# Joined products in a Strassen feed-forward: matmuls sorted by columns, a fourth joined product, and sums moved to GpSimd

## What is computed

```python
xn2 = rms_norm(h, norm2_w[l])
h = h + (jax.nn.silu(xn2 @ w_ffn_gate[l]) * (xn2 @ w_ffn_up[l])) @ w_ffn_down[l]
return rms_norm(h, final_norm_w)
```

## Time and profile before

| | us |
|---|---|
| median of 3 runs | 815.28 (815.2 to 820.14) |
| profiled execution | 815.42 |
| its span, first to last instruction | 813.7 |
| TensorE matmuls busy in it | 807.3 (99%) |
| VectorE | 561.7 (69%) |
| ScalarE | 441.3 (54%) |
| GpSimd | 413.6 (51%) |

### The profile page before, as it was taken

One profiled execution on the slowest core, in us unless ns is written; L12 is line 12 of the kernel. 1 busy time (PEld: TensorE's weight loads), 2 busy tenths in 40 slices (PEclk: granted clock), 3 DMA queues, 4 the chain that ended last, 5 costly groups with the idle time before them and its releaser, 6 DMA issues.

```text
span 813.7 us, 12790 instructions
## 1 busy us (share of the span) xinstructions
PE 807.3 (99%) x5192; PEld 734.2 (90%) x5192; DVE 561.7 (69%) x600; ACT 441.3 (54%) x501; POOL 413.6 (51%) x146
## 2 busy tenths in 40 slices
PE   9999999999999999999999999999999999999997
PEld 8888888888888899999998899999999999999985
DVE  5377377364774957888974278777778888878836
ACT  5523446756665645867442575544555446665624
POOL 3545424424224543477955443544444445878880
PEclk9999999999999999999999999999999999999999
DMA  8972422131122253322235302332234445536022
GB/s 290 269 272 107 158 101 101 55 103 53 52 104 106 102 207 105 104 104 105 84 131 204 104 1 104 136 108 109 109 110 160 161 159 188 183 121 216 2 77 104
DMA packets 29869, 103.11 MB, mean 127 GB/s; under 512 B 2816, under 2 KB 7296, under 8 KB 25856
## 3 DMA queue, kind: packets, MB, share of 16 engines
q1 hardware_dynamic: 24592, 87.07, 30.1%
q10 hardware_dynamic: 5232, 15.40, 6.0%
HBM read 94.08 MB, written 8.39 MB: 126 GB/s over the span
## 4 chain that ended last, share of the span: by engine, by line
PE 99%; ACT 0%; issue 0%; DVE 0%; ACTq 0%
PE acc L2170 11%; PE acc L2172 11%; PE acc L2173 11%; PE acc L1955 7%; PE acc L1957 6%; PE acc L1956 6%; PE acc L2182 6%; PE acc L1972 6%; PE acc L1973 6%; PE acc L1974 6%; PE acc L2184 3%; PE acc L2400 3%; PE acc L2001 3%; PE acc L2388 2%; PE acc L2390 2%; PE acc L2391 2%
## 5 line engine op out<-in xcount | busy, mean ns | idle before, releaser
L489 POOL TENSOR_TENSOR w_lo<-raw,w_hi 128x2048 fp32r<-128x2048 f32 x26 | 122.7, 4718 | 163.3 <-ACT w_hi L684 163.3
L510 POOL TENSOR_TENSOR A_lo<-wp,A_hi 128x1024 fp32r<-128x1024 f32 x51 | 126.0, 2470 | 144.3 <-ACT A_hi L859 137.2
L874 ACT ACTIVATE S_hi<-acc 128x1024 fp32r<-128x1024 f32 x68 | 68.1, 1025 | 90.2 <-PE acc L2173 39.7
L1477 DVE TENSOR_TENSOR S_lo<-acc,S_hi 128x1024 fp32r<-128x1024 f32 x68 | 81.7, 1219 | 14.2 <-ACT S_hi L874 14.1
L1955 PE MATMUL acc<-xt_hi,w_hi 128*128 128x512 f32 x224 | 88.0, 393 | 0.0
L1957 PE MATMUL acc<-xt_hi,w_lo 128*128 128x512 f32 x224 | 87.2, 389 | 0.0
L1956 PE MATMUL acc<-xt_lo,w_hi 128*128 128x512 f32 x224 | 87.2, 389 | 0.0
L684 ACT ACTIVATE w_hi<-raw 128x2048 fp32r<-128x2048 f32 x26 | 49.6, 1910 | 63.9 <-PE acc L1974 43.5
L859 ACT ACTIVATE A_hi<-wp 128x1024 fp32r<-128x1024 f32 x51 | 53.8, 1054 | 17.6 <-PE acc L2173 17.6
L2182 PE MATMUL acc<-ft,A_hi 128*128 128x512 f32 x144 | 51.7, 399 | 0.0
L1957 PEld LDWEIGHTS acc<-xt_hi,w_lo 128*128 128x128 f32 x224 | 42.0, 188 | 8.8
(11 more groups left out here) (362 smaller groups left out, 2608.6 us busy)
## 6 DMA issues: line engine op xcount, KB each, us to landing
wp<-wstream SPq DMA_DIRECT2D x34, 1024.0 KB, 7.0
raw<-wstream SPq DMA_DIRECT2D x26, 1024.0 KB, 4.8
wd<-wstream SPq DMA_DIRECT2D x16, 512.0 KB, 6.2
down_sums<-act_sum ACTq DMA_DIRECT2D x8, 512.0 KB, 3.2
sum_raw<-down_sums SPq DMA_DIRECT2D x8, 512.0 KB, 3.8
xn_in<-x ACTq DMA_DIRECT2D x4, 512.0 KB, 8.3
turned_sums<-tx ACTq DMA_DIRECT2D x4, 512.0 KB, 3.9
raw_out<-wstream SPq DMA_DIRECT2D x2, 1024.0 KB, 5.8
```

The costliest lines, as they stand in the source:

```text
L489: pool.tensor_tensor(w_lo[s][:, :], raw[s][:, :], w_hi[s][:, :], ALU.subtract).then_inc(lo_ready, 1)
L510: pool.tensor_tensor(low_of(name, rows), weights_of(name, c, rows), high_of(name, rows), ALU.subtract).then_inc(plain_low, 1)
L874: a.activation(high_of(name, rows), src, ACT.Copy).then_inc(op_high, 1)
L1477: v.tensor_tensor(low_of(name, rows), src, high_of(name, rows), ALU.subtract).then_inc(s_low, 1)
```

## The change

1. In `wide_product` and `wide_down_product` all matmuls of 512 columns come first, then all of 256 columns.
2. In pairs 9 to 17 four products are joined: A11 and S2 in banks 6 and 7 (now `SPARE`), S3 and A22 in banks 1 and 2 (`LAST_ROW`). A12 is plain, in bank 0; S1 and S4 are plain in bank 3. The down pairs keep their three joined products and their banks.
3. u3 and C21 are joined by two VectorE instructions each, C11 by one straight from bank 0 without ScalarE's copy. P1's join moves ahead of S4's forming.
4. The high and the low part of S3 come before C21 and before S1's, in pairs 8 to 16.
5. TensorE: A11 waits for a low part of S (S3's, since it uses those banks), S1 for the second one; S2 waits for P1's join; A12 for the C11 of the pair before; the first down pair's A11 also for C21 of pair 17.
6. `act_sums` moves from VectorE to GpSimd, at the end of GpSimd's pair.

```diff
-        FIRST_ROW, SECOND_SUM = (0, 1), (6, 7)
+        FIRST_ROW, LAST_ROW, SPARE = (0, 1), (1, 2), (6, 7)
...
+            def act_sums(q):
+                m = (q - FIRST_SUMS) // 2
...
+                if q == FIRST_SUMS:
+                    pool.wait_ge(act_ready, 2)
+                    pool.wait_ge(pair_ready, 3)
+                    pool.tensor_tensor(t1, x12, x11, ALU.subtract).then_inc(t_formed, 1)
+                    pool.wait_ge(t_formed, A_FORMED + 1)
+                    pool.tensor_tensor(t2, x22, t1, ALU.subtract).then_inc(t_formed, 1)
...
                 pair((None, p), p % 2)
+                if p < LAST_FFN:
+                    act_sums(p - MERGE_PAIRS)
...
-                    a.activation(by_bank(p1), low_sums(FIRST_ROW), ACT.Copy).then_inc(low_taken, 1)
+                    a.wait_ge(joined, at(p, 5, 1 - 10))
+                    a.wait_ge(taken, at(p, 2, -2))
+                    a.activation(by_bank(p1), low_sums(SPARE if spare else FIRST_ROW), ACT.Copy).then_inc(low_taken, 1)
...
-                take_c11(p, first)
+                if first:
+                    take_first_c11(p)
+                if not rows:
+                    s_high("S3", diff, at(p, 4, 2))
...
                 a.wait_ge(product_done, at(p, 7, 6 - 7))
                 s_high("S1", chain, at(p, 4, 1), rows)
-                s_high("S3", diff, at(p, 4, 2), rows)
+                if rows:
+                    s_high("S3", diff, at(p, 4, 2), rows)
...
             def join_c11(p):
-                v.wait_ge(low_taken, at(p, 2, -2 * NARROW_PAIRS))
-                v.tensor_tensor(cq[:, 0, :, :], high_sums(FIRST_ROW), cq[:, 0, :, :], ALU.add).then_inc(taken, 1)
+                v.wait_ge(product_done, at(p, 7, 5 - 7))
+                v.wait_ge(taken, at(p, 2, -1))
+                quarter(0, 0, p1).then_inc(taken, 1)
...
-            def join_u3(p):
+            def join_u3(p, b=None):
...
+                if b is not None:
+                    v.tensor_tensor(u3[:, :], bank[b][:, :], u2[:, :], ALU.add).then_inc(joined, 1)
+                else:
+                    join_wide(by_bank(u3), LAST_ROW, by_bank(u2), at(p, 3, -1 - 3 * NARROW_PAIRS)).then_inc(joined, 1)
...
                     s_low_of("S2", chain, at(p, 7, 5 - 7))
+                    join_p1(p)
                     v.wait_ge(s_low, at(p, 4, 3 - 4))
                     form_s4(c)
-                if not first:
-                    join_p1(p)
...
-                if q is not None and q != PAIRS:
-                    act_sums(q)
-                join_c21(p)
-                s_low_of("S1", chain, at(p, 7, 2), rows)
-                if q != PAIRS:
-                    s_low_of("S3", diff, at(p, 7, 3), rows)
-                v.wait_ge(s_low, at(p, 4, 1))
+                if not rows:
+                    s_low_of("S3", diff, at(p, 7, 2))
+                join_c21(p, first)
+                s_low_of("S1", chain, at(p, 7, 2 if rows else 3), rows)
+                v.wait_ge(s_low, at(p, 4, 1 if rows else 2))
...
                     for k in range(4):
                         pe.matmul(bank[banks[g]][:, :], wh[:, g, k, :], both[:, k, :], start=(start and k == 0), stop=False,
                                   skip_group_check=True)
+                for g in range(2):
+                    for k in range(4):
                         mm = pe.matmul(bank[banks[g]][:, 0:HT], wl[:, g, k, :], both[:, k, 0:HT], start=False, stop=(k == 3),
                                        skip_group_check=True)
...
-                    wide_product("A11", f11, FIRST_ROW, True)
-
-                pe.wait_ge(s_low, p * 4 + (1 - 4))
+                    pe.wait_ge(s_low, p * 4 + (1 - 4))
+                    wide_product("A11", f11, SPARE, True)
...
+                    pe.wait_ge(s_low, p * 4 + (2 - 4))
                     pe.wait_ge(joined, p * 5 - 5)
-                product("S1", t1, 2, True)
+                product("S1", t1, 3, True)
...
-                    wide_product("S2", tb[1], SECOND_SUM, True)
+                    pe.wait_ge(taken, p * 2 - 1)
+                    wide_product("S2", tb[1], SPARE, True)
...
+                else:
+                    wide_product("S3", tb[2], LAST_ROW, True)
...
-                    wide_product("A12", f21, FIRST_ROW, False)
+                    pe.wait_ge(taken, p * 2 - 2)
+                product("A12", x21, 0, not first)
...
+                    wide_product("A22", f12, LAST_ROW, False)
...
-                product("S4", x22, 2, False)
+                product("S4", x22, 3, False)
...
                 pe.wait_ge(taken, 2 * p - 2)
+                if p == LAST_FFN + 1:
+                    pe.wait_ge(joined, 5 * LAST_FFN - 1)
```

More of the change, by code:

```diff
@@ L78 @@
 NARROW_PAIRS = MERGE_PAIRS + 1
+FOUR_WIDE = LAST_FFN - NARROW_PAIRS
 LAST_PAIR = LAST_FFN + DOWN_PAIRS
@@ L1071, in pair_silu, with take_p1 @@
                 a.activation(silp[:, :, :], cq[:, :, 0, :], ACT.Silu).then_inc(silp_ready, 1)
-            def take_p1(p, first=False):
+            def take_p1(p, first=False, spare=True):
                 a.wait_ge(product_done, at(p, 7, 1 - 7))
-                if not first:
-                    a.wait_ge(joined, at(p, 5, 1 - 10))
                 if first:
@@ L1079, in take_p1, with take_first_c11 @@
                 else:
-                    a.activation(by_bank(p1), low_sums(FIRST_ROW), ACT.Copy).then_inc(low_taken, 1)
-            def take_c11(p, first=False):
+                    a.wait_ge(joined, at(p, 5, 1 - 10))
+                    a.wait_ge(taken, at(p, 2, -2))
+                    a.activation(by_bank(p1), low_sums(SPARE if spare else FIRST_ROW), ACT.Copy).then_inc(low_taken, 1)
+            def take_first_c11(p):
                 a.wait_ge(product_done, at(p, 7, 5 - 7))
[L1084 to L1089, removed]
+                a.activation(cq[:, 0, :, :], bank[0][:, :].rearrange("p (g t) -> p g t", g=2), ACT.Copy).then_inc(taken, 1)
             def act_high(m, s):
@@ L1727, in join_u2 @@
                 else:
[L1728 to L1730 removed]
+                    join_wide(by_bank(u2), SPARE, by_bank(p1), joins or at(p, 3, -2 - 3 * NARROW_PAIRS)).then_inc(joined, 1)
+            def join_u3(p, b=None):
                 v.wait_ge(product_done, at(p, 7, 4 - 7))
                 v.wait_ge(joined, at(p, 5, 1 - 5))
[L1733 removed]
+                if b is not None:
+                    v.tensor_tensor(u3[:, :], bank[b][:, :], u2[:, :], ALU.add).then_inc(joined, 1)
+                else:
+                    join_wide(by_bank(u3), LAST_ROW, by_bank(u2), at(p, 3, -1 - 3 * NARROW_PAIRS)).then_inc(joined, 1)
             def quarter(n, b, u):
@@ L1742, in join_c22, with join_c21 @@
                 v.wait_ge(joined, at(p, 5, 2 - 5))
-                quarter(3, 2, u3).then_inc(joined, 1)
-            def join_c21(p):
+                quarter(3, 3, u3).then_inc(joined, 1)
+            def join_c21(p, first=False):
                 v.wait_ge(product_done, at(p, 7, 6 - 7))
-                quarter(2, 3, u2).then_inc(joined, 1)
+                if first:
+                    quarter(2, 2, u2).then_inc(joined, 1)
+                else:
+                    join_wide(cq[:, 2, :, :], LAST_ROW, by_bank(u2), at(p, 3, -3 * NARROW_PAIRS)).then_inc(joined, 1)
             def join_c12(p):
                 v.wait_ge(product_done, at(p, 7))
-                quarter(1, 2, u2).then_inc(joined, 1)
+                quarter(1, 3, u2).then_inc(joined, 1)
             def act_low(m, s):
@@ L1795, in pair @@
                     s_low_of("S2", chain, at(p, 7, 5 - 7))
+                    join_p1(p)
                     v.wait_ge(s_low, at(p, 4, 3 - 4))
                     form_s4(c)
-                if not first:
-                    join_p1(p)
                 join_u2(p, first)
                 if first:
-                    join_u3(p)
+                    join_u3(p, 2)
                 s_low_of("S4", chain, at(p, 7))
@@ L2355, in pair @@
                     pe.wait_ge(t_low, N_LOW + 3)
-                    pe.wait_ge(act_ready, 2)
-                product("S3", t3, 3, True)
+                    product("S3", t3, 2, True)
+                else:
+                    wide_product("S3", tb[2], LAST_ROW, True)
                 pe.wait_ge(plain_low, p * 3 - 1)
-                pe.wait_ge(taken, p * 2 - 1)
                 if first:
-                    product("A12", x21, 0, False)
+                    pe.wait_ge(taken, p * 2 - 1)
                 else:
-                    wide_product("A12", f21, FIRST_ROW, False)
+                    pe.wait_ge(taken, p * 2 - 2)
+                product("A12", x21, 0, not first)
                 pe.wait_ge(plain_low, p * 3)
@@ L2369, in pair @@
                     pe.wait_ge(t_low, N_LOW + 4)
-                product("A22", t4, 3, False)
+                    product("A22", t4, 2, False)
+                else:
+                    wide_product("A22", f12, LAST_ROW, False)
                 pe.wait_ge(s_low, p * 4)
                 pe.wait_ge(joined, p * 5 + (3 - 5))
```

(13 more changed lines are left out.)

68 lines of the change are left out of this document (31 added, 37 removed).

## The result

The changed kernel takes 818.79 us (median of 20 runs, 818.25 to 820.24) against 815.32 for the kernel before: ratio 1.0043, 95% interval 1.0037 to 1.0049. It is slower by 3.5 us, where 0.2 us less was forecast, and 0.8 us outside the range.

The account below looks back on a forecast made before the run. TensorE, 99% of the chain of waits, was taken as the bound. 815.42 - 2.8 (work) + 1.5 (looped pairs) + 1.1 (last feed-forward pair) = 815.2, set to 815.1 for the median; range 814.2 to 816.3, with rivals 812.4 to 818.0.

Parts of the forecast that it names:

- TensorE's work: 39 sorted joined products at 2.78 us instead of 2.83, nine newly joined at 2.78 instead of 2.88: 2.8 us less together.
- The rule that I set against it: TensorE's matmuls: about 2.5 ns fixed cost each, making the whole change 0.2 us of work instead of 2.8.
- The looped pairs: S1 of eight following pairs awaits VectorE's C12, TensorE late by 0.19 us each: 1.5 us.
- The chain: VectorE's queue from the end of S2 through C12, laid out at 14.13 us; S1's weight load due at 13.98.
- u3's second half: Ends 5.62 us after S2, A22's load due at 5.54: late by 0.12, inside the 0.19, not added.
- The last feed-forward pair: Two added halves in VectorE's queue delay C21, so the first down pair's A11 is 1.1 us late, once.
- bounds of 0.4 and 1.8: First down pair's A11 lateness: 0.4 us without GpSimd blocking VectorE's low part, 1.8 if blocked twice; 1.1 taken.
- The down pairs: Their 3 x 4 joined products save 0.05 us each by sorting; no stall inside these pairs was counted.
- GpSimd's sums: Eight sums at GpSimd's pair ends, 4.8 us a pair: cost nothing, 1 us in hand; otherwise under 1 us.
- P1's join: Now awaited by S2: ends at 16.5 us, S2 due at 17.2, so covered with 0.7 us in hand.
- Rival C: VectorE's chain becomes the period, at C12 before S1: 0.35 us more a pair, 817.9 us; chance 0.22.

## Why the prediction was wrong

**TensorE's work: right in kind, a quarter too large.** 2.78 forecast for a sorted joined product, 2.79 measured; 19.76 forecast for a pair without stalls, 19.81 measured. Such hundredths stand in each of thirteen pairs: 0.19 saved in nine and about 0.10 in four make 2.1 us, not the 2.8 of the sum. The rule that I set against it, a fixed 2.5 ns for each matmul (the Trainium skill, TensorE: Matmul & The Clock Gate, "Wait — 56ns, not 53.3ns?"), would have left nothing to gain by sorting; sorting alone gives 0.2%, so the measurement decides against it for these float32 operands.

**The looped pairs: right in place, near in size.** The forecast was 0.19 in each of eight, 1.5 us. Measured are 0.1, 0.1, 0.6, 0.1 and 0.2 in pairs 9 to 13 and none in pairs 14 to 17, 1.1 us. The chain has the length laid out: 13.12 us from u2 to C12 inside the loop, 13.16 forecast (14.13 - 0.29 - 0.68), and forming S3 earlier takes 0.8 of the 1.1 away. But the total is near by luck. S1 waits for C12 only where VectorE's program passes the end of a turn of its loop, 0.5 us ahead of pair 11 and 0.1 ahead of pair 13, which the prediction did not have. In pairs 9, 10 and 12 the 0.1 stand ahead of A22, behind u3's second half (0.12 forecast), and give C12 the time it lacked: in pair 12 it ends at 578.64, and S1's load starts at 578.69 without a wait.

**The last feed-forward pair: the step that failed.** The prediction had A11 of the first down pair 1.1 us late, with bounds of 0.4 and 1.8, and 2.28 were measured. The parts of the queue were right: without the exclusion the two added halves cost 0.43. What I mis-sized was VectorE's low parts. I saw one of them blocked for 0.7 us and carried that 0.7 over. But a block is no property of the instruction; it depends on which engine comes first, and here the first low part escaped and the second lost 1.85. The change itself had moved GpSimd: without C11's copy on ScalarE its operation came 1.6 us earlier in the pair, as the two traces show, and the prediction counted that removal as nothing. The traces show what a meeting costs: 3.07 with GpSimd's operation under way, 1.21 with it held back. The rule that I quoted (the Trainium skill, SBUF — State Buffer, "Who interferes with whom") adds that issue order decides who blocks, and the traces agree: 1.21 when VectorE's came first, 3.07 when GpSimd's did. The 2.4 us of GpSimd's operation are then the bound for each meeting; by my estimate from the rows two meetings would have made the upper bound about 5 (0.4 + 2 x 2.4), not 1.8.

**The down pairs: left out, the second step that failed.** I counted their shorter products and put their stalls at nothing, since the change leaves VectorE's work there alone. 1.8 us were lost in the third by the same exclusion, because VectorE's instruction came 0.2 us later against its pair. Holding GpSimd back there removes it. Where the 0.2 us come from is open: VectorE forms S1 behind a copy of ScalarE (of A21) that starts 0.4 us after the end of u2 where it was 0.1, and no run tells why.

**The half clock: not thought of.** Some executions pay 1.6 us more behind the long stall. It is no part of the 3.5: the profiled execution of the changed kernel took 818.80 and has no such stretch.

**GpSimd's sums and P1's join: right,** both cost TensorE no wait. Rival C named the right sign and nearly the time (817.9), but its place is refuted: with the looped pairs' stalls gone the kernel is still slower than before, and with the two late losses gone it is level.

The account: 2.1 us of work less, 1.1 of stalls in the looped pairs, 2.3 ahead of the first down pair, 1.8 in the third and 0.3 before the stage make 3.4 us, the difference of the two spans. The forecast had 2.8 less, 1.5, 1.1, nothing and nothing.

## What to carry to other kernels

When one engine's queue is lengthened, or another's is shortened, list every instruction of it that reads two operands from SBUF and every GpSimd operation that may be under way then: each meeting can cost nearly GpSimd's whole operation (2.2 of 2.4 us here), and a shift of 0.2 us decides it, also in stages that the change does not touch. A wait that lets the engine on the critical path go first cost no stall here and made the order firm. A new wait on the engine that is the bound deserves its own layout for each special pair, the last above all.

## What the runs showed of the hardware

- VectorE's low part of 128 x 1024 with both inputs in SBUF took 1.21 to 1.22 us alone and 1.3 to 3.44 when GpSimd's operation had begun first, by how much of it was left; GpSimd's took up to 3.4 instead of 2.4 in its turn, in the kernel before (5.79 for the two from 727.32 on).
- A matmul costs about 13 ns beside its columns here (0.227 us for 512, 0.120 for 256), and changing from 512 to 256 columns and back 5 ns more: 2.83 against 2.79 us for eight of each.
- 2.3 us without matmuls were followed by a stretch at 1.2 GHz in some executions and not in others of one kernel; stalls of 0.43 and 1.1 us were not, in the traces taken.
